# Gated linear attention in four unrolled rounds of six projection tiles, with query and key decayed straight from the accumulator

## The reference

```python
def gla_chunked(q, k, v, log_alpha):          # c = 64
    qc = q * dk ** -0.5
    cum = cumsum(log_alpha within a chunk); cum_last = cum at the chunk's end
    q_t = qc * exp(cum)
    k_t = kc * exp(-cum)
    a = where(causal, q_t @ k_t.T, 0)
    intra = a @ vc
    contrib = (kc * exp(cum_last - cum)).T @ vc
    state = exp(cum_last) * state + contrib   # from chunk to chunk
    inter = q_t @ state_before_the_chunk
    return intra + inter

def odd_mixer(hn, w_in, w_alpha, b_alpha, out_gain, w_out):
    g_q, g_k, g_v, g_r, g_a = split(hn @ w_in)
    log_alpha = log_sigmoid(g_a @ w_alpha + b_alpha) / 16
    o = gla_chunked(heads of g_q, g_k, g_v, log_alpha)
    return (rms_norm(o, out_gain) * silu(g_r)) @ w_out
```

## Time and profile before

| | us |
|---|---|
| median of three runs | 2160.03 (2154.52 to 2162.74) |
| profiled execution | 2159.55 |
| its span | 2157.8 |
| PE busy | 2003.5 (93%) |
| DVE busy | 1141.2 (53%) |
| POOL busy | 821.1 (38%) |
| ACT busy | 697.1 (32%) |

### The profile page before, as it was taken

How to read it: one execution, slowest core, us unless ns; L and a number is a source line. 1 busy time by engine, 2 the same in 40 slices (tenths; PEclk the granted TensorE clock), 3 DMA queues, 4 the chain that set the end, 5 groups by cost and what they waited for, 6 DMA issues and landing times.

```text
span 2157.8 us, 27917 instructions
## 1 busy us (share of the span) xinstructions
PE 2003.5 (93%) x9960; PEld 1573.1 (73%) x9960; DVE 1141.2 (53%) x1995; ACT 697.1 (32%) x1284; POOL 821.1 (38%) x428
## 2 busy tenths in 40 slices
PE   4999999787999997999998999999998898999999
PEld 4877777666777875666677888887586676888887
DVE  5728998676995434555535555412514435555411
ACT  2125656223552114445414333200313424333200
POOL 1451221244774442222234444444242134444443
PEclk9999999898999998999999999999999999999999
DMA  3630100221202322111122322233121122222232
GB/s 118 169 114 30 40 30 30 69 70 54 64 32 67 98 89 82 49 59 59 50 78 80 97 97 95 93 107 116 60 88 49 39 69 80 97 95 94 95 125 78
DMA packets 55149, 167.56 MB, mean 78 GB/s; under 512 B 8064, under 2 KB 16128, under 8 KB 54800
## 3 DMA queue, kind: packets, MB, share of 16 engines
q1 hardware_dynamic: 47760, 155.22, 22.1%
q10 hardware_dynamic: 7296, 11.08, 1.8%
HBM read 157.88 MB, written 2.10 MB: 74 GB/s over the span
## 4 chain that ended last, share of the span: by engine, by line
PE 63%; issue 16%; DVE 14%; POOL 4%; ACT 1%; ACTq 1%; DMA 0%; DVEq 0%; POOLq 0%
PE bank L177 14%; PE bank L179 14%; PE bank L178 14%; POOL wlo L160 4%; PE bank L332 2%; PE bank L333 2%; PE bank L334 2%; DVE prob L1498 2%; DVE ssb L1485 2%; PE bank L2345 1%; PE bank L2347 1%; PE bank L2346 1%; DVE sb__137 L2160 1%; DVE wtmp L1938 1%; DVE sb__137 L2155 1%
## 5 line engine op out<-in xcount | busy, mean ns | idle before, releaser
L160 POOL TENSOR_TENSOR wlo<-raw,whi 128x1024 fp32r<-128x1024 f32 x244 | 587.1, 2407 | 999.8 <-DVE whi L168 999.8
L168 DVE CAST whi<-raw 128x1024 fp32r<-128x1024 f32 x288 | 202.6, 704 | 632.7 <-PE bank L179 442.6
L177 PE MATMUL bank<-xh,whi 128*128 128x512 f32 x832 | 326.9, 393 | 11.8 <-POOL wlo L160 9.0
L179 PE MATMUL bank<-xh,wlo 128*128 128x512 f32 x832 | 325.9, 392 | 0.0
L178 PE MATMUL bank<-xl,whi 128*128 128x512 f32 x832 | 325.8, 392 | 0.0
L177 PEld LDWEIGHTS bank<-xh,whi 128*128 128x128 f32 x832 | 157.5, 189 | 47.5 <-POOL wlo L160 10.7
L178 PEld LDWEIGHTS bank<-xl,whi 128*128 128x128 f32 x832 | 157.5, 189 | 32.6
L179 PEld LDWEIGHTS bank<-xh,wlo 128*128 128x128 f32 x832 | 157.3, 189 | 32.8
L573 PE MATMUL bank<-xh,whi 128*128 128x512 f32 x328 | 140.8, 429 | 2.2 <-ACT oin L559 1.2
L177 PE MATMUL bank<-ghi,whi 128*128 128x512 f32 x352 | 136.9, 389 | 0.0
L178 PE MATMUL bank<-glo,whi 128*128 128x512 f32 x352 | 136.9, 389 | 0.0
(11 more groups left out here) (370 smaller groups left out, 3975.1 us busy)
## 6 DMA issues: line engine op xcount, KB each, us to landing
raw<-in_weights_dram SPq DMA_DIRECT2D x288, 512.0 KB, 3.6
h<-in_x_dram SPq DMA_DIRECT2D x1, 2048.0 KB, 8.3
sz<-su SPq DMA_DIRECT2D x128, 16.0 KB, 1.8
out_dram<-h ACTq DMA_DIRECT2D x4, 512.0 KB, 3.4
etab<-in_even_tables_dram ACTq DMA_DIRECT2D x1, 1730.0 KB, 6.5
x_kh<-kvc_h ACTq DMA_DIRECT2D x2, 256.0 KB, 4.2
x_kl<-kvc_l ACTq DMA_DIRECT2D x2, 256.0 KB, 5.6
x_vh<-kvc_h ACTq DMA_DIRECT2D x2, 256.0 KB, 8.4
```

The source lines that it names most:

```text
L160: nc.gpsimd.tensor_tensor(wlo[:, s % 2, :], raw[:, s, :], whi[:, s % 2, :].bitcast(F32), ALU.subtract).then_inc(w_lo, 1)
L168: nc.vector.tensor_copy(whi[:, t_of_4 % 2, :], raw[:, t_of_4, :]).then_inc(w_hi, 1)
L177: nc.tensor.matmul(to, w_h, pe_h, start=first and k == 0, stop=False)
L179: last_mm = nc.tensor.matmul(to, w_l, pe_h, start=False, stop=last and k == chunks - 1)
```

## The change

The 24 input tiles come in another order: four rounds of six tiles, first value, query, key and output gate of head 0, and so on (`ODD`). The host lays the weights out in that order. Each round computes one head, in straight code without loops.

- Query and key are no longer copied to `oin`. DVE makes `qt`, `kt` and `kd` from the accumulator (`dve_decayed`), and this frees it. Value is turned a tile at a time and taken straight to `vo`; the output gate goes through Silu straight from the accumulator to `ogate`. `oin` and the copies from it are gone.
- The head's output stands in banks 6 and 7, the scores in bank 4, the transposed key in bank 5, and the contributions in banks 2 and 3, in two rounds, of four chunks and three.
- The products within the chunks come first, all in a row, and then the seven steps from the states.
- Between the steps of round i stand two quarters each of its output gate tiles, and behind the output the value, query and key tiles of round i+1.
- In the last round, 12 of the 16 chunks of the first two output tiles stand behind the output, so that the output product begins before the last head is finished.
- The decays of round 0 are taken after two of four heads' cumulated gates, and the splits of the weights have new places on DVE.

```diff
...
+        def pe_out_rest(pe, stage, begun, hi, lo, n):
...
             for m in range(KC):
...
+                    pe.wait_ge(w_lo, T0[stage] + m + 1)
+                    pe.wait_ge(acc_free[m % 2], (O0[stage] + m) // 2 + 1)
+                for k in range(begun if m < 2 else 0, KC):
+                    mm = pe_out_chunk(pe, m, k, hi, lo)
                 mm.then_inc(tile_done, 1)
...
-        oin = at("oin", [P, 24, S])
...
+        ohi = at("ohi", [P, KC, S], F32R)
+        olo = at("olo", [P, KC, S], F32R)
...
+        ogate = at("ogate", [P, 2, S])
...
+        ODD = ("va", "vb", "q", "k", "ra", "rb")
...
-            return bank[2 + 2 * (c % 2) + c // 4][:, half * 2 * P:(half + 1) * 2 * P]
+            return bank[2 + c % 2][:, half * 2 * P:(half + 1) * 2 * P]
+        def pe_turn_values(pe, e, i):
+            odd_taken(pe, ODD[e], i)
+            for b in range(4):
+                mm = nc.tensor.transpose(bank[2 + e][:, b * P:(b + 1) * P], sq[:, e, b * P:(b + 1) * P], ident)
+            mm.then_inc(tv_turned, 1)
...
-            products_from_norm(pe, "odd_in", n, gate, gate_up)
-            products_feature_major(pe, "odd_in", 4, 4)
...
+                if j == 2:
+                    pe.wait_ge(o_mn, 2)
+                    pe.wait_ge(o_ab, 2)
+                    for e in range(2):
+                        pe_turn_values(pe, e, 0)
+            products_from_norm(pe, "odd_in", n, gate, behind_tile)
+            parts = iter(range(16, 24 * 4))
+            def beside(count):
+                for _ in range(count):
+                    product_beside(pe, "odd_in", 0, 0, 4, next(parts))
             pe.wait_ge(o_mn, 8)
-            products_token_major(pe, "odd_in", 8, 8)
-            pe.wait_ge(tv_taken, TV0["odd_in"] + 8)
-            with pe.Fori(0, 2) as ii:
...
-            beside(0, 1, 2)
-            pe.wait_ge(o_qk, nth(i, 3, 1))
+            pe.wait_ge(o_ab, 8)
+            for i in range(4):
+                pe_odd_head(pe, i, beside)
+        def pe_odd_head(pe, i, beside):
+            beside(2)
+            odd_taken(pe, "q", i)
+            odd_taken(pe, "k", i)
+            if i:
...
-                mm = nc.tensor.matmul(bank[6][:, b * P:(b + 1) * P], kt[:, b * P:(b + 1) * P],
+                mm = nc.tensor.matmul(bank[4][:, b * P:(b + 1) * P], kt[:, b * P:(b + 1) * P],
...
-            beside(3)
-            pe.wait_ge(o_qk, nth(i, 3, 2))
+            if i:
+                pe.wait_ge(o_kt, i)
             for b in range(4):
...
+            beside(2)
+            pe.wait_ge(o_kt, i + 1)
+            pe.wait_ge(tv_taken, TV0["odd_in"] + 2 * i + 2)
+            pe_contributions(pe, i, range(4))
+            beside(2)
+            pe.wait_ge(o_s, 7 * i + 4)
+            pe_contributions(pe, i, range(4, NCH - 1))
+            beside(2)
+            pe.wait_ge(o_am, i + 2)
+            if i:
+                pe.wait_ge(o_m, 2 * i)
             for b in range(4):
...
+                    nc.tensor.matmul(bank[6 + e][:, b * P:(b + 1) * P], vo[:, e, b * P:(b + 1) * P],
+                                     att[:, b * P:(b + 1) * P], start=b == 0, stop=False)
+            for c in range(1, NCH):
+                pe.wait_ge(o_s, 7 * i + c)
+                for e in range(2):
+                    mm = nc.tensor.matmul(bank[6 + e][:, c * CH:(c + 1) * CH], state[:, c - 1, e * P:(e + 1) * P],
+                                          qt[:, c * CH:(c + 1) * CH], start=False, stop=c == NCH - 1)
             mm.then_inc(o_o, 1)
+            if i < 3:
+                beside(1)
+            else:
+                pe_odd_out_chunks(pe, 0, 2)
             for e in range(2):
...
+            if i < 3:
+                beside(5)
+                pe_turn_values(pe, 0, i + 1)
+                beside(4)
+                pe_turn_values(pe, 1, i + 1)
+                beside(6)
+            else:
+                pe_odd_out_chunks(pe, 2, 12)
...
+        def pe_contributions(pe, i, chunks):
...
+        def pe_odd_out_chunks(pe, first, last):
+            for m, k in [(m, k) for m in range(2) for k in range(6)][first:last]:
+                if k == 0:
+                    pe.wait_ge(w_lo, T0["odd_out"] + m + 1)
+                    pe.wait_ge(acc_free[m], (O0["odd_out"] + m) // 2 + 1)
+                pe.wait_ge(o_lo, k + 1)
+                pe_out_chunk(pe, m, k, ohi, olo)
+        def pe_odd_out(pe, n):
+            pe.wait_ge(o_lo, 8)
+            pe_out_rest(pe, "odd_out", 6, ohi, olo, n)
...
+        def act_take_values(act, e, i):
+            act.wait_ge(tv_turned, TV0["odd_in"] + 2 * i + e + 1)
+            nc.scalar.activation(vo[:, e, :], bank[2 + e][:], ACT.Copy).then_inc(tv_taken, 1)
...
+            act_odd_tile(act, "va", 0, sq[:, 0, :])
...
-                take_beside(act, "odd_in", 0, 0, 4, hd, lambda: oin[:, hd, :])
-            act_take(act, "odd_in", 4, 4, oin, lambda i, j: i * 2 + (4 + j))
-            act_take_turned(act, "odd_in", 8, 8, oin, 16)
...
+            act_alpha(act, 0)
+            act_alpha(act, 1)
+            act_odd_tile(act, "vb", 0, sq[:, 1, :])
+            act_decays(act, 0)
+            act_alpha(act, 2)
+            act_alpha(act, 3)
+            for e in range(2):
+                act_take_values(act, e, 0)
+            for i in range(4):
+                act_odd_head(act, i)
...
+        def act_odd_head(act, i):
+            act.wait_ge(o_tr, i + 1)
+            nc.scalar.activation(kdt[:], bank[5][:], ACT.Copy).then_inc(o_kt, 1)
+            for e in range(2):
+                act_odd_tile(act, ("ra", "rb")[e], i, ogate[:, e, :], ACT.Silu)
...
-            take_beside(act, "odd_in", 16, ii, 4, 2 * hh, lambda: tile_of(oin, i * 2 + 8), alone=bank[7])
...
+            act.wait_ge(o_o, i + 1)
...
+                nc.scalar.activation(osq[:, e, :], bank[6 + e][:], ACT.Square).then_inc(o_sq, 1)
...
+            if i < 3:
+                act_decays(act, i + 1)
...
+                act.wait_ge(o_mix, 2 * i + e + 1)
+                nc.scalar.activation(ohi[:, 2 * i + e, :], omix[:, e, :], ACT.Copy).then_inc(o_hi, 1)
+            if i < 3:
+                for e in range(2):
+                    act_odd_tile(act, ODD[e], i + 1, sq[:, e, :])
+                    act_take_values(act, e, i + 1)
...
+        def dve_decayed(dve, i):
...
+            t = T0["odd_in"] + odd_tile("q", i)
+            dve.wait_ge(o_e, 3 * i + 3)
+            dve.wait_ge(tile_done, t + 1)
+            nc.vector.scalar_tensor_tensor(qt[:], acc[0][:], float(P) ** -0.5, oe[:, 0, :],
+                                           ALU.mult, ALU.mult).then_inc(acc_free[0], 1)
+            dve_odd_split(dve, "q", i)
+            dve.wait_ge(tile_done, t + 2)
+            nc.vector.tensor_tensor(kt[:], acc[1][:], oe[:, 1, :], ALU.mult)
+            nc.vector.tensor_tensor(kd[:], acc[1][:], oe[:, 2, :], ALU.mult).then_inc(acc_free[1], 1)
+            dve_odd_split(dve, "k", i)
...
+        def dve_odd(dve):
+            nc.vector.memset(att[:], 0.0).then_inc(o_am, 1)
+            dve_odd_split(dve, "va", 0)
+            dve_alpha(dve, 0)
+            dve_until_end(dve, 0)
+            dve_alpha(dve, 1)
+            dve_odd_split(dve, "vb", 0)
+            dve_alpha(dve, 2)
+            dve_alpha(dve, 3)
+            dve_decayed(dve, 0)
+            for i in range(4):
+                dve_odd_head(dve, i)
...
+        def dve_states(dve, i, chunks):
+            for c in chunks:
+                if c == 0:
+                    nc.vector.tensor_copy(state[:, 0, :], of_chunk(c)).then_inc(o_s, 1)
...
+                    nc.vector.scalar_tensor_tensor(state[:, c, :], state[:, c - 1, :],
+                                                   oe[:, 0, (c + 1) * CH - 1:(c + 1) * CH], of_chunk(c),
+                                                   ALU.mult, ALU.add).then_inc(o_s, 1)
...
+        def dve_odd_head(dve, i):
+            dve.wait_ge(o_at, i + 1)
+            nc.vector.copy_predicated(att[:], causal.bitcast(mybir.dt.uint32), bank[4][:]).then_inc(o_am, 1)
+            if i < 3:
+                dve_until_end(dve, i + 1)
+            dve_odd_split(dve, "ra", i)
+            dve.wait_ge(o_c, 7 * i + 4)
+            dve_states(dve, i, range(4))
+            dve.wait_ge(o_c, 7 * i + 7)
+            dve_states(dve, i, range(4, NCH - 1))
+            dve_odd_split(dve, "rb", i)
+            dve.wait_ge(o_r, i + 1)
...
-            nc.vector.scalar_tensor_tensor(qt[:], tile_of(oin, i), float(P) ** -0.5, oe[:, 0, :],
...
-            nc.vector.tensor_tensor(kt[:], tile_of(oin, i + 4), oe[:, 1, :], ALU.mult).then_inc(o_qk, 1)
...
-            dve.wait_ge(o_e, nth(i, 3, 2))
...
+                nc.vector.scalar_tensor_tensor(omix[:, e, :], bank[6 + e][:], obias[:, 4 + e:5 + e], orr[:],
...
+                odd_taken(dve, ("ra", "rb")[e], i)
+                nc.vector.tensor_tensor(omix[:, e, :], omix[:, e, :], ogate[:, e, :], ALU.mult).then_inc(o_mix, 1)
+            if i < 3:
+                dve_odd_split(dve, "va", i + 1)
```

(15 more changed lines are left out.)

210 lines of the change are left out of this document (67 added, 143 removed).

## The result

| | before | after |
|---|---|---|
| median, us | 2159.37 (2154.52 to 2162.74, 4 runs) | 2127.54 (2125.42 to 2129.07, 4 runs) |
| ratio, with 95% interval | | 0.9861 (0.9847 to 0.9875) |
| profiled execution | 2159.55 | 2128.43 |
| its span | 2157.8 | 2126.3 |
| odd block, second input tile to last output product | 249.8 | 222.3 |

The kernel became 31.8 us faster; 2133 us (2124 to 2147) were forecast. In the two profiled executions 27.5 of 31.5 us of span lie in the odd block, where 26.9 were forecast, nothing lies behind it, and 3.9 us lie ahead of it, for which the sum had no term. The experiments come back to these 3.9.

A forecast was written before the change was run, and what follows sets the result against it. PE, busy 93% of the span, was taken as the bound, with waits and low clock at head borders; the odd block's terms summed to 222.9 us instead of 249.8, 26.9 less, so 2133 us (2124 to 2147).

The forecast's parts named there:

- The border of heads: Odd block, between heads: three PE waits of 4.4 us for `kt`, with the low clock behind them, go.
- a series of some 10 us over ACT and DVE, with three quarters of a tile to cover it: From sum of squares through `omix` and `olo` to the next head's `kt`, with 4.1 us of cover.
- Rounds: Odd block, scores to scores: no PE wait in the steady round, 44.9 us each; 44.5 to 46 as sign of right.
- the turn of a value: PE's transposes of the value in each head: 0.6 us each plus 0.1 for going back to products, eight in all.
- the stop at the third output tile: Output product, where the third tile's split and POOL come late: a new loss of 2.0 us, nothing for clock.
- the row of the even block: Even block's output product: a stop of 2.5 us left the granted clock at 1.00, so none was priced.
- Start: First gate tile, its split behind the cumulated gates and `qt`: a new PE wait of 1.25 us, 0 to 2.5.
- the walk: One round followed by earlier durations: slack of 0.6 us at the states and 1.7 at the turned value.
- New waits inside the rounds: Rival: DVE instructions held by POOL cost PE 7 to 14 us in the rounds; 2140 to 2147 us; chance 0.16.
- The held instruction that it feared: DVE's two `olo` held by the next value tile's low part on POOL: up to 2.4 us later, not in the last round.
- The cover does not cover: Rival: PE stands at the value's turn about 6 us, three times; 18 of 27 us return; 2151 us; chance 0.05.
- The weights come late: Rival: late splits start gate or value tiles 3.1 us late; at twelve tiles 27 us slower, 2187 us; chance 0.04.

The follow-up runs named there:

- e_hoist: Kernel before in straight code, with the next head's decays, `vo`, `qt` and `kt` made right behind the output's products: 2139.21 us, ratio 0.9913.
- e_unroll: Kernel before with its loop over heads written out as straight code on PE, ACT and DVE: 2153.96 us, ratio 0.9981.
- e_late_out: Changed kernel with all 12 early chunks of the output product moved behind the last head: 2134.71 us, ratio 0.9898.
- c_after: The changed kernel run again with nothing altered: 2128.50 us, ratio 0.9877.
- e_chain: Changed kernel with four ACT copies that feed nothing put ahead of the norm factor's logarithm in each round: 2132.85 us, ratio 0.9889.
- e_start: Changed kernel with the split behind the first query tile issued ahead of the last cumulated gate on DVE: 2128.03 us, ratio 0.9877.
- e_chain8: Changed kernel with eight ACT copies that feed nothing put ahead of the norm factor's logarithm in each round: 2143.28 us, ratio 0.9933.

## Why the prediction was right, and where it was off

**The mechanism held.** The border of heads was worth what its rows said. Taking it away with the layout as before (e_hoist) gave 20.6 of the 27.5 us: 13.3 of waits, 6.9 of low clock behind them, and 0.4 by the straight code. The larger gain of e_unroll, 5.4 us, is mostly clock at places where e_hoist ran like the kernel before, and is no part of the 20.6. So the words "a series of some 10 us over ACT and DVE, with three quarters of a tile to cover it" name the cause; six-tile rounds, own banks and direct decays are one way to cure it and not the only one. The output product begun early is worth 5.5 us (e_late_out, from the first scores on). Set beside the 6.9 us between e_hoist and the changed kernel, that leaves some 1.4 us for six-tile rounds, own banks and direct decays by themselves; this is a difference of single executions, and no run has these parts alone.

**The terms of the sum.**

| stretch of the block | forecast | measured |
|---|---|---|
| second input tile to first scores (7.2 + 10.9 + 1.3 + 1.25 + 2.7) | 23.35 | 23.48 |
| three rounds | 134.7 | 132.72 |
| last scores to last output product | 64.85 | 66.09 |
| sum | 222.9 | 222.3 |

- *Rounds:* 44.24 us instead of 44.9. The mis-sized term is the turn of a value. I took 0.6 us, the time for which the earlier trace rows show four transposes, and 0.1 for going back to products. But the shown time runs to the end of the last one, and the next product starts earlier. The turn in the trace after:

```profile
1624.32 0.60 PE L1652 MATMUL bank<-tables,sq 128*128 128x128 f32 x4
1624.67 0.48 PE L573 MATMUL bank<-xh,whi 128*128 128x512 f32 x1
1624.99 0.40 PE L574 MATMUL bank<-xl,whi 128*128 128x512 f32 x1
```

  It costs 0.35 from start to start and (0.32 - 0.23) = 0.1 for the return: 0.45, not 0.7. Twice a round that is 0.5 us; the other 0.2 are spread over the head's own work, 10.7 for 10.9. I had read all other terms as distances of starts, and this one as a shown duration. So the rounds lie just below the 44.5 to 46 us that I had given as a sign of being right.
- *End:* the stop at the third output tile cost 1717.54 - 1715.29 - 0.23 = 2.0 us from start to start, as forecast, and 1.6 us of clock on top. By the row of the even block, where 2.53 us of stop left the clock at 1.00, I had put nothing for the clock. The rule that I set beside it, from the Trainium skill (TensorE: Matmul & The Clock Gate, "What's actually happening"), has windows that run free of the kernel; that a stop may fall either way by where they lie is what I made of it, and would have put in 1 to 2 us. The runs agree with that: the same 1.86 us at the same instruction brought the low clock in three executions (the first profile, c_after and e_chain) and not in a fourth (e_start). That a stop as short as this brings it at all stands on these runs, and not on the Trainium skill. A stop's length alone did not decide it, and the one row of a stop without low clock was weak evidence for another.
- *Start:* 1.51 us for 1.25. The scan ended at 1546.25, 16.6 us behind the second tile's start at 1529.64 (16.7 in the walk), and the first gate tile started 20.6 us behind it (20.5), so the step held. The wait is longer because PE came to it earlier: the first two turns cost 0.9 us and not 1.3, the same mis-sized term.
- These errors have both signs and cancel: 0.6 us in 222.9 is better than the terms deserve. The rest of the difference between 2133 and the measured median, some 5 us, lies ahead of the block (3.9) and in the spread of executions. The last output product, forecast near 1756 us of the span, ended at 1751.9 for the same reason. The sum had nothing for this, and the range held it only by the spread that was added to it; without those 4 us its lower end would have been 2128.
- Two figures of the forecast are slips on which nothing else rests. Twelve chunks of the output product are 36 products at 0.23, 8.2 us and not 16; and 2139 with half the spread of 8 us is 2143 and not 2141.

**The rivals.** "New waits inside the rounds" did not come, and not by luck: the room was 0.8 us at the states and 1.5 at the value (0.6 and 1.7 in the walk), and e_chain shows that the room at the value is real; the one at the states was not tried. The held instruction that it feared did appear, in the one place named for it. The `olo` pair took 3.48 us beside POOL's subtraction, 1.29 in the last round where no split stands in front of it. This is as the rule of the Trainium skill (SBUF — State Buffer, "Who interferes with whom") had it. The pair ended at 1625.9, and nothing on PE asked for it before the scores of 1641.6. "The cover does not cover" needed ACT late by 7.7 us; e_chain8 shows what it would look like at 4.2. "The weights come late" did not come: the rounds have no wait for `wlo`.

## What to carry to other kernels

When the busiest engine stops at a border of a loop, follow the series on the other engines between its last product and its next need, and count what work stands beside it; moving what the next step needs ahead of what only the end needs can give most of the gain without another layout. Read the room of each hand-over in the trace as a distance (last end to next need): it is an amount that can be spent, and at the two places tried here it was exact to 0.2 us. Price small instructions of a pipelined engine by the distance between starts, and compare versions by the stretch that changed, since the total carries several microseconds of clock that the change did not make. Look for such clock inside the stretch too: here it hid 1.6 of the 5.5 us of e_late_out.

## What the runs showed of the hardware

- The same stop of PE, 1.86 us at the same instruction, was followed by some 4 us at half clock in three executions and by full clock at once in one: 1.6 us that no edit explains. The stop of 2.95 us at the output product was followed by it in three (both of the kernel before, and e_hoist) and not in e_unroll. In e_chain8 stops of 2.6 us at three equal places were followed by it twice (0.96 for the round) and once not (1.00 in the third).
- Ahead of the block, with identical code, executions differ by up to 7.8 us (1527.4 to 1535.2 us) with low clock in other places.
- Where DVE's pair `olo<-omix,ohi` and POOL's subtraction ran together, POOL was held as well: 2.77 us instead of 2.4.

```profile
1622.57 2.77 POOL L160 TENSOR_TENSOR wlo<-raw,whi 128x1024 fp32r<-128x1024 f32 x1 [9.79 <-DVE whi L168]
```

  DVE lost 2.2 us in that encounter and POOL 0.4. Of DVE's pair, which started 0.17 us ahead of POOL, the first took 0.68 us and the second 2.88; the same happened in all three rounds that have a split there, and not in the last. The delay of POOL is small but not nothing, where its low part is what a tile waits for.
- The same hold can reach PE: in e_start it made DVE's `omin<-omin,oa` 2.33 us long instead of 0.69, and PE waited 0.36 us for `qt` behind it.
